# Seven block products in place of eight in eight of the sixteen weight tiles of two down-projections

## The reference, cut to what matters

```python
def squared_relu_mlp(n, w_up, w_down):          # n: 256 x 1024, w_up: 1024 x 4096, w_down: 4096 x 1024
    return jnp.square(jax.nn.relu(n @ w_up)) @ w_down
# in layer 0 and 1:
h = h + squared_relu_mlp(rmsnorm(h, g_ffn[layer]), w_up[layer], w_down[layer])
```

## Time and profile before

| | us |
|---|---|
| median of 3 runs (lowest, highest) | 959.05 (958.77, 959.27) |
| the profiled execution | 958.25 |
| its span | 956.4 |
| TensorE busy | 947.5 |
| VectorE busy | 612.2 |
| ScalarE busy | 546.2 |
| GpSimd busy | 134.6 |

### The profile page before, as it was taken

How to read it: one execution, slowest core, us unless ns; L and a number is a source line. 1 busy time by engine, 2 the same in 40 slices (tenths; PEclk the granted TensorE clock), 3 DMA queues, 4 the chain that set the end, 5 groups by cost and what they waited for, 6 DMA issues and landing times.

```text
span 956.4 us, 14401 instructions
## 1 busy us (share of the span) xinstructions
PE 947.5 (99%) x5992; PEld 841.5 (88%) x5992; DVE 612.2 (64%) x890; ACT 546.2 (57%) x779; POOL 134.6 (14%) x44
## 2 busy tenths in 40 slices
PE   9999999999999999999999999999999999999997
PEld 7888888888888888888888888899999999999886
DVE  5897747776222667747777522486558699888643
ACT  7676447666333658847666333635465687665542
POOL 0021250001664000020000665300000000000000
PEclk9999999999999999999999999999999999999999
DMA  8653244554555452445544555364444435545541
GB/s 306 233 188 141 91 155 177 196 177 176 210 186 210 158 204 88 177 146 185 199 177 176 199 197 183 137 220 177 156 157 168 182 155 186 208 180 177 190 163 44
DMA packets 25344, 168.21 MB, mean 176 GB/s; under 512 B 2816, under 2 KB 3904, under 8 KB 5568
## 3 DMA queue, kind: packets, MB, share of 16 engines
q1 hardware_dynamic: 24848, 166.84, 48.4%
q10 hardware_dynamic: 432, 0.46, 0.2%
HBM read 166.24 MB, written 1.05 MB: 175 GB/s over the span
## 4 chain that ended last, share of the span: by engine, by line
PE 94%; ACT 2%; DVE 2%; issue 1%; POOL 0%; DVEq 0%; ACTq 0%; POOLq 0%
PE bank L680 23%; PE bank L681 23%; PE bank L682 23%; PE bank L762 12%; PE bank L766 6%; PE bank L708 1%; DVE wlo L1874 1%; ACT whi L1256 1%; PE bank L816 0%; PE bank L1035 0%; ACT nhl L1268 0%; PE bank L1169 0%; PE bank L800 0%; PE bank L820 0%; PE bank L824 0%
## 5 line engine op out<-in xcount | busy, mean ns | idle before, releaser
L1874 DVE TENSOR_TENSOR wlo<-raw,whi 128x2048 fp32r<-128x2048 f32 (+2 forms) x151 | 309.4, 2049 | 249.7 <-ACT whi L1256 249.7
L1256 ACT ACTIVATE whi<-raw 128x2048 fp32r<-128x2048 f32 (+1 forms) x154 | 293.4, 1906 | 151.4 <-PE bank L682 149.7
L2606 POOL TENSOR_TENSOR wlo<-raw,whi 128x1024 fp32r<-128x1024 f32 (+1 forms) x38 | 133.1, 3506 | 472.4 <-ACT whi L1256 465.0
L762 PE MATMUL bank<-nhl,whi 128*128 128x512 f32 x512 | 124.3, 392 | 0.2 <-DVE nhl L1887 0.2
L762 PEld LDWEIGHTS bank<-nhl,whi 128*128 128x128 f32 x512 | 93.9, 188 | 19.4 <-issue 0.7
L680 PE MATMUL bank<-mhi,whi 128*128 128x258 f32 x384 | 108.6, 283 | 0.0
L681 PE MATMUL bank<-mlo,whi 128*128 128x258 f32 x384 | 108.3, 282 | 0.0
L682 PE MATMUL bank<-mhi,wlo 128*128 128x258 f32 x384 | 108.2, 282 | 0.0
L680 PE MATMUL bank<-nhl,whi 128*128 128x258 f32 (+3 forms) x320 | 92.3, 288 | 0.8 <-DVE wlo L1874 0.8
L681 PE MATMUL bank<-nhl,whi 128*128 128x258 f32 (+3 forms) x320 | 91.4, 286 | 0.0
L682 PE MATMUL bank<-nhl,wlo 128*128 128x258 f32 (+3 forms) x320 | 90.5, 283 | 0.0
(11 more groups left out here) (329 smaller groups left out, 1737.1 us busy)
## 6 DMA issues: line engine op xcount, KB each, us to landing
raw<-w_stream SPq DMA_DIRECT2D x154, 1024.0 KB, 4.8
h<-x_rows SPq DMA_DIRECT2D x4, 256.0 KB, 4.4
raw<-w_stream SPq DMA_DIRECT2D x2, 512.0 KB, 5.7
cst<-consts SPq DMA_DIRECT2D x1, 832.0 KB, 6.4
e<-g_post SPq DMA_DIRECT2D x1, 512.0 KB, 3.3
out_rows<-e SPq DMA_DIRECT2D x2, 256.0 KB, 2.0
raw<-w_stream SPq DMA_DIRECT2D x1, 352.0 KB, 8.9
vec<-vectors SPq DMA_DIRECT2D x1, 258.5 KB, 8.4
```

Of the source, the lines that this page charges most:

```text
L762: return pe.matmul(us[c].t[:, :], w[:, k, c * P:c * P + P].hi, nboth[:, k, :], start=k == 0, stop=k == 7)
L1256: act.activation(whi[j][:, 0:n], raw[j][:, 0:n], ACT.Copy).then_inc(s_hi.up(i))
L1874: dve.tensor_tensor(wlo[j][:, 0:m], raw[j][:, 0:m], whi[j][:, 0:m].bitcast(F32), ALU.subtract).then_inc(s_lod.up(i))
L2606: pool.tensor_tensor(wlo[j][:, m:n], raw[j][:, m:n], whi[j][:, m:n].bitcast(F32), ALU.subtract).then_inc(s_lop.up(i))
```

## The change

The two halves of rows and of columns of a weight tile make four blocks, and with the two halves of the tokens a tile is a product of 2 x 2 blocks by 2 x 2 blocks. In tiles 2, 3, 5, 6, 8, 9, 11 and 12 of both down-projections (`SEVEN`) it is made with seven block products instead of eight:

- **VectorE** makes three combinations of weight blocks from `raw` (`combined`: 1024 columns, and two times 512) for the tile two ahead, and their low parts (`combined_lo`: two times 1024 columns) one tile later. `lo` makes only 512 columns of such a tile.
- **ScalarE** rounds the combinations (`combined_hi`: two times 1024 columns; there is one buffer for each, so it waits until TensorE has used the one before). `hi` leaves out the 512 columns of the right upper block, in two instructions.
- **GpSimd** makes, during the up-projection, four sums of token blocks of 128 columns for each of the eight blocks of features (`row_sums`), and after ScalarE's rounding (`sums_hi`, in the up-projection three turns later) their low parts of 128 and 384 columns. It keeps its 1024 columns of each weight tile's low part. VectorE's `joined` of turn m waits until the sums of m - 2 are made, as they are read from the same buffer.
- **TensorE** runs `seven_products` for these tiles. Four more banks gather sums that belong to several outputs; the slot of the weight tile is given back after the third of the seven products.
- **At the end**, `seven_1` and `seven_2` spread these four banks over `h` on VectorE during tiles 13 and 14.
- **SP** loads a tile into a slot when `combined` has read the one before, too.

```diff
+SEVEN = (2, 3, 5, 6, 8, 9, 11, 12)
...
+            def seven_products(l, it, us):
+                q = SEVEN.index(it)
+                first, final = q == 0, q == len(SEVEN) - 1
+                p1, p5, p6, p7 = (begin("st", l, j) if first else use["st", l, j] for j in range(4))
+                w = weights(DOWN[l] + it, 2)
+                a, s = FF[l][:, 2 * it:2 * it + 2, :], ASP[q]
+                ta, tb = TW
+                on.wait_ge(*s_fflo.at(l, it))
+                weights_in(DOWN[l] + it)
+                x = mm3(p1.t[:, :], a[:, 0, 0:P], w[:, 0, 0:512], first, final)
+                if final:
+                    x.then_inc(p1.full)
+                mm3(us[0].t[:, :], a[:, 1, 0:P], w[:, 1, 0:512], False, False)
+                on.wait_ge(*s_aslo.at(l, q))
+                mm3(us[1].t[:, :], s[:, 2 * P:3 * P], w[:, 1, 512:1024], False, False).then_inc(us[3].full)
+                on.wait_ge(*s_tlo.at(l, q, 0))
+                x = mm3(p5.t[:, :], a[:, 0, P:2 * P], ta[:, 0:512], first, final)
+                if final:
+                    x.then_inc(p5.full)
+                mm3(p7.t[:, :], s[:, P:2 * P], ta[:, 512:1024], first, final).then_inc(p7.full)
+                on.wait_ge(*s_tlo.at(l, q, 1))
+                mm3(p6.t[:, :], s[:, 0:P], tb[:, 0:512], first, final)
+                mm3(us[2].t[:, :], a[:, 1, P:2 * P], tb[:, 512:1024], False, False).then_inc(p6.full)
...
                 for it in range(n):
                     if before:
                         before(it)
+                    if seven_at(tile + it):
+                        seven_products(s // 2, it, us)
+                        continue
...
+                if seven_at(i):
+                    act.activation(whi[j][:, 0:512], raw[j][:, 0:512], ACT.Copy)
+                    act.activation(whi[j][:, 1024:2048], raw[j][:, 1024:2048], ACT.Copy).then_inc(s_hi.up(i))
+                    return
...
+            def sums_hi(l, m):
+                q = SEVEN.index(m)
+                on.wait_ge(*s_as.at(l, q))
+                act.activation(FF[l].hi[:, 2 * m, P:2 * P], AS[:, 0:P], ACT.Copy)
+                act.activation(ASP[q].hi, AS[:, P:4 * P], ACT.Copy).then_inc(s_ashi.up(l, q))
+
+            def combined_hi(l, it):
+                q = SEVEN.index(it)
+                for part in range(2):
+                    on.wait_ge(*s_ts.at(l, q, part))
+                    if q:
+                        on.wait_ge(*use["st", l, 3 - part].done(q - 1))
+                    act.activation(TH[part], TX[part], ACT.Copy).then_inc(s_thi.up(l, q, part))
+
+            def down_hi(l, it):
+                if it + 1 in SEVEN and it not in SEVEN:
+                    combined_hi(l, it + 1)
+                hi(DOWN[l] + it + 2)
+                if it + 1 in SEVEN and it in SEVEN:
+                    combined_hi(l, it + 1)
+                if it == SEVEN[-1] + 1:
+                    u = use["st", l, 2]
+                    on.wait_ge(*u.done(len(SEVEN) - 1))
+                    act.activation(EX[0], u.t[:, :], ACT.Copy).then_inc(u.free)
...
-                j, m = i % NSLOT, cuts[i]
+                j, m = i % NSLOT, 512 if seven_at(i) else cuts[i]
...
+            def combined(l, it):
+                q, i = SEVEN.index(it), DOWN[l] + it
+                r = raw[i % NSLOT]
+                right, above = r.rearrange("p (k c n) -> p k c n", k=2, c=2)[:, :, 1, :], r[:, 0:1024].rearrange("p (k n) -> p k n", k=2)
+                on.wait_ge(s_raw[i % NSLOT], 16 * (i // NSLOT + 1))
+                if q:
+                    on.wait_ge(*s_tlo.at(l, q - 1, 1))
+                dve.tensor_tensor(TX[0].rearrange("p (k n) -> p k n", k=2), right, above, ALU.subtract).then_inc(s_ts.up(l, q, 0))
+                on.wait_ge(*s_ts.at(l, q, 0))
+                dve.tensor_tensor(TX[1][:, 0:512], r[:, 1536:2048], TX[0][:, 0:512], ALU.subtract).then_inc(own.up())
+                on.wait_ge(*own.last())
+                dve.tensor_tensor(TX[1][:, 512:1024], r[:, 1024:1536], TX[1][:, 0:512], ALU.subtract).then_inc(s_ts.up(l, q, 1))
+
+            def combined_lo(l, it):
+                q = SEVEN.index(it)
+                if q == 0:
+                    on.wait_ge(*s_aslo.at(l, len(SEVEN) - 1))
+                for part in range(2):
+                    on.wait_ge(*s_thi.at(l, q, part))
+                    dve.tensor_tensor(TL[part], TX[part], TH[part].bitcast(F32), ALU.subtract).then_inc(s_tlo.up(l, q, part))
+
+            def down_lo(l, it):
+                if it in SEVEN:
+                    lo(DOWN[l] + it + 2)
+                if it + 1 in SEVEN:
+                    combined_lo(l, it + 1)
+                if it + 2 in SEVEN:
+                    combined(l, it + 2)
+                if it not in SEVEN:
+                    lo(DOWN[l] + it + 2)
+
+            def seven_1(l, factor):
...
+            def seven_2(l, factor):
...
                 def joined(m, c):
                     u = use["up", l, m, c]
+                    if m - 2 in SEVEN:
+                        on.wait_ge(*s_as.at(l, SEVEN.index(m - 2)))
...
+            def row_sums(l):
+                for q, m in enumerate(SEVEN):
+                    x = SQR[l][m % 2]
+                    a11, a21, a12, a22 = (x[:, i * P:i * P + P] for i in range(4))
+                    s1, s2, s3, s4 = (AS[:, i * P:i * P + P] for i in range(4))
+                    on.wait_ge(*s_fflo.at(l, m))
+                    if q:
+                        on.wait_ge(*own.last())
+                        on.wait_ge(*s_aslo.at(l, q - 1))
+                    pool.tensor_tensor(s1, a21, a22, ALU.add).then_inc(own.up())
+                    pool.tensor_tensor(s3, a11, a21, ALU.subtract).then_inc(own.up())
+                    on.wait_ge(own.sem, own.n - 1)
+                    pool.tensor_tensor(s2, s1, a11, ALU.subtract).then_inc(own.up())
+                    on.wait_ge(*own.last())
+                    pool.tensor_tensor(s4, a12, s2, ALU.subtract).then_inc(s_as.up(l, q))
+                    on.wait_ge(*s_ashi.at(l, q))
+                    pool.tensor_tensor(FF[l].lo[:, 2 * m, P:2 * P], s1, FF[l].hi[:, 2 * m, P:2 * P].bitcast(F32), ALU.subtract).then_inc(own.up())
+                    pool.tensor_tensor(ASP[q].lo, AS[:, P:4 * P], ASP[q].hi.bitcast(F32), ALU.subtract).then_inc(s_aslo.up(l, q))
+
             for i in range(2, NTILE):
                 j, m, n = i % NSLOT, cuts[i], sizes[i]
+                if i - 2 in DOWN:
+                    row_sums(DOWN.index(i - 2))
...
+                        if seven_at(i - NSLOT):
+                            on.wait_ge(*s_ts.at(*seven_at(i - NSLOT), 1))
```

More of the change, by code:

```diff
@@ L230, with seven_at @@
 SECOND_DFT = {4: 0, 8: 1, 12: 2, 14: 3}
+SEVEN = (2, 3, 5, 6, 8, 9, 11, 12)
 PROJ = [0, 5, 7, 9, 11, 13] + [C0 + 2 * i for i in range(6)]
 NTILE = 156
+def seven_at(i):
+    for l in range(2):
+        if i - DOWN[l] in SEVEN:
+            return l, SEVEN.index(i - DOWN[l])
+    return None
 def cut(i):
@@ L281, in proj, with out @@
             last[PROJ[p] + half] = (("pj", p, 1), half)
-    def out(s, tile, n, inner=(), turn=None):
+    def out(s, tile, n, inner=(), turn=None, seven=False):
         for j in range(4):
@@ L287, in out @@
             banks.take(*name)
+        if seven:
+            for j in range(4):
+                banks.take("st", s // 2, j, hold=True, signals=1 if j < 2 else len(SEVEN))
+            for j in range(4):
+                banks.drop("st", s // 2, j)
         for j in (0, 2, 1):
@@ L357, in plan_banks @@
     mlp(0, 1)
-    out(1, DOWN[0], 16, (), 2)
+    out(1, DOWN[0], 16, (), 2, True)
     def steps(p, q):
@@ L367, in plan_banks @@
     banks.take("metaT")
-    out(3, DOWN[1], 16, (), 4)
+    out(3, DOWN[1], 16, (), 4, True)
     for m in range(2):
@@ L453, in block_kernel @@
         h = sb("h", 2 * D).rearrange("p (t n) -> p t n", t=2)
+        o_nhl = place[0]
         nhl = sb("nhl", 8 * 2 * L2, F32R)
@@ L550, in block_kernel @@
             FFP.append(A.pair(32 * S))
+            o_sqr = A.at
             SQR.append([A(512), A(512)])
             HALVES.append(A(512))
-            assert A.at <= o_meta
+            AS = A(512)
+            o_as = A.at
         FF = [f.view("p (k t) -> p k t", k=32) for f in FFP]
+        TX = [at(f"tr{i}", 1024, o_nhl + 4096 * i) for i in range(2)]
+        TH = [at(f"th{i}", 1024, o_nhl + 8192 + 4096 * i, F32R) for i in range(2)]
+        TL = [at(f"tl{i}", 1024, o_sqr + 4096 * i, F32R) for i in range(2)]
+        TW = [Pair(TH[i], TL[i]) for i in range(2)]
+        EX = [at(f"ex{i}", 512, o_sqr + 2048 * i) for i in range(4)]
+        o_sums = [o_xn + 3072 * i for i in range(5)] + [o_as + 3072 * i for i in range(3)]
+        ASP = [Pair(at(f"ash{i}", 3 * P, o, F32R), at(f"asl{i}", 3 * P, o + 1536, F32R)) for i, o in enumerate(o_sums)]
+        assert o_sums[4] + 3072 <= o_clo + 8 * N2 * 4 and o_sums[7] + 3072 <= o_meta
         A = Area("c")
@@ L642, in block_kernel @@
```

(56 more changed lines are left out.)

2 lines of the change are left out of this document (1 added, 1 removed).

## The result

The changed kernel takes 988.24 us (median of 4; 987.52 to 988.95), the kernel before 959.12 beside it. The ratio is 1.0304, 95% interval 1.0292 to 1.0316: slower, by 29.1 us. The forecast was 985 (964 to 1000). The profiled execution took 988.95 us with a span of 987.1.

What follows compares the result with a forecast made beforehand. TensorE bounds the kernel (busy 947.5 of 956.4 us). Two stages losing 12.1 + 1.0 each, matmul saving included, add 26.2 to 958.25: 984.5 for the profiled execution, 985 as the median; range 964 to 1000.

Steps and rivals of the forecast that it cites:

- The collision: Down stages: VectorE instructions with two SBUF inputs and GpSimd instructions run one after the other, each whole.
- The period: Down stages, three tiles: shared work 11.9 of VectorE plus 6.9 of GpSimd, 18.8 us, against 15.0 of TensorE.
- The start of a stage: Down stage: VectorE free at 236.0; tile 3 ends at 26.4 us, where TensorE alone would be at 20.4.
- The lag from the up-projection: VectorE's lag left at the up-projection's end delays its down-stage start one for one: 1 us, bounds 0 and 4.
- The last of the three periods: Down stage: after tile 3, three periods of 18.8 us each bring tile 13 to 82.8.
- The up-projections: GpSimd's sums take 2.9 us; three turns take 16.8 against 16.7; VectorE's lag costs TensorE nothing there.
- What hides: Down stages: `seven_1`, `seven_2` beside other work, 14 of 16.3 us, cost 0, up to 2; ScalarE, weight transfers 0.
- The first (948, no collision): Down stages: VectorE's 11.9 stays under 15.0, the whole 10.9 us comes out, 948; chance 0.10.
- The second (a collision that the slack takes up, 15.6 to 17.2 us a period): Down stages: GpSimd slips into VectorE's waits; -3.0 to +3.4 us a stage, 953 to 966; chance 0.10.
- The third (999): Up-projections: GpSimd's small instructions make 19.0 for 16.7 us, down stage starts 5 us later, 999; chance 0.10.

Runs made afterwards that it cites:

- the tail experiment: Changed kernel with the last three tiles of the second down stage's look-ahead made whole on VectorE; 986.75 us, ratio 1.0287 to the kernel before.

## Why the prediction was right, step by step

- **The collision** was the mechanism forecast, and it is shown: by the stretched rows, by -37.4 us when the half is left out, by -24.9 when it moves to the busier engine, and by the fill that costs nothing.
- **The period** was forecast as 18.8 and measured 18.70, and it carried the forecast. That it is so close is luck, for two terms were off and cancel. The three excesses of 2.1 us make 6.3 for GpSimd, where 6.9 was put: half of the 4.62 us for 2048 columns was too much. The other 12.4 are VectorE's, where 11.9 was put: undisturbed, `combined` takes 2.58 us start to start (279.75 to 282.33) for 2.48, and the two low parts 2.54 (282.33 to 284.87) for 2.30.
- **The start of a stage** had an error in each direction. The lag from the up-projection was put at 1.0 us and is 3.5 (`combined` begins 7.5 us after the first matmul, at 239.85, not 5.0). The last of the three periods was put at 18.8 but is 16.5 (VectorE's last low part of tile 9 ends at 297.92, that of tile 12 at 314.43), since one GpSimd instruction of it falls behind the tile that TensorE waits for. 12.1 + 1.0 was forecast, 13.2 measured in the first stage; this too is luck, the agreement is closer than the terms deserve.
- **The up-projections** cost nothing in their own time, as forecast: TensorE's longest wait there is 0.2 us. But GpSimd's six instructions for one set of sums take about 3.7 us, not 2.9: those on 128 columns lie 0.42 us apart, start to start, and the one on 384 takes 1.47. The lag comes from the wait in `joined`, 1.73 us of VectorE idle in every third turn. After the first of these waits (`joined` at 179.92; the turns before it lie 5.57 us apart, the last at 171.59) VectorE is already 2.8 us late. From there three turns take it 17.05 us (179.92 to 196.97) for TensorE's 16.7.
- **The second stage** is where the sum failed by 3.3 us. "What hides" put the end at 0, up to 2 if its cover went. It weighed the first stage, whose last tiles VectorE makes whole, and not the second, where GpSimd works on until the end (by the same terms 5.6 + 3 x 1.15 + 3 x 2.3 = 16.0 of 16.3 us) and VectorE makes one more low part before the adds. VectorE's last `lo` takes 3.44 us there, and TensorE waits 2.3 us for `h` (timelines of VectorE and TensorE):

```profile
630.20 3.44 DVE L1960 TENSOR_TENSOR wlo<-raw,whi 128x1024 fp32r<-128x1024 f32 x1 [0.15 <-ACT whi L1316]
...
634.45 1.22 PE L737 MATMUL bank<-vec,h 128*128 128x128 f32 x8 [2.29 <-DVE h L2264]
```

- **The clock** had no term. TensorE's granted clock went from 2.4 to 1.2 GHz three times between the first down-projection and the end of the second: it reads 0.78 in 244 to 249 and 0.88 in 249 to 254 (one stretch at half clock), 0.72 in 545 to 550, and 0.72 in 634 to 640. Matmuls of 512 columns then start 0.43 us apart instead of 0.227 (247.04 to 247.46). What it costs inside the stages is not shown; VectorE is late there anyhow, so it is probably little. Behind the last wait, four spacings of 0.43 (636.02 to 637.73) make 0.8 us of the second stage, and seven of 272 columns, 0.23 for 0.125, make 0.7 of the +0.9 behind it, which is gone where the clock stays (the tail experiment).
- **The rivals**: the first (948, no collision) is near what the kernel does when GpSimd only fills, 950.7. The second (a collision that the slack takes up, 15.6 to 17.2 us a period) is ruled out by 18.70. The third (999) was nearly right on its price, 3.7 us for 4.0 a set, and wrong on what follows: 17.05 us in three turns where it had 19.0.
- **Slips that changed nothing**: 19.4 + 1.15 + 2.3 + 2.3 is 25.15, not 25.0; the losses of 19.1 a stage give 997, not 998; and the VectorE row with a PSUM operand in the earlier trace rows lies inside GpSimd's for 0.57 of its 0.75 us, not for all of it.

## What to carry to other kernels

Add the GpSimd and the VectorE time of a stage when the instructions of both read two SBUF tensors, and hold the sum, not each engine, against the bound. A share of elementwise work that GpSimd makes at half of VectorE's speed is not a relief then: here it took 2.1 us of VectorE's time to save 1.15. It was free here only because VectorE had nothing else to do, and it had to be taken back before VectorE was given more.

## What the runs showed of the hardware that I had not expected

- A busy time can be waiting. In the period above GpSimd's row of 6.12 us for two instructions holds some 1.5 us in which VectorE's instructions go first (6.12 less twice 2.3), and VectorE's busy 95.5 us of 101.2 hold three times 2.1 us a period of GpSimd's. What tells them apart is a second row of the same shape.
- The length of a wait does not tell whether TensorE's clock falls after it. In the changed kernel it fell to half after waits of 2.04 us (before 245.47), 1.92 (before 545.91) and 2.29 (before 634.45), but not after the longer ones of 2.90 (before 255.03; 254 to 259 reads 1.00) and 3.09 (before 555.67). In the tail experiment it did fall after the same wait there, 3.12 us (0.79 in 555 to 560). With VectorE making all low parts a wait of 1.99 us (before 540.63) was followed by 1.00, and the kernel before, with no such waits, reads 1.00. What decides it is open.
- The order of arrival by 0.2 us decides who waits: the same pair of halves costs VectorE 1.22 us when it starts first, or 3.29 when GpSimd does.
